# Token mixes of an RWKV-7 layer: residual moved out of memory for a while, second low-rank factors in three rounded passes between the passes of the next mix, operand splits released feature tile by feature tile

## What is computed

```python
x_prev = concatenate([shift0[:, None, :], h[:, :-1]], axis=1)
xx = x_prev - h
xr, xw, xk, xv, xa, xg = [h + xx * mix[i] for i in range(6)]
r = xr @ w_r
k = xk @ w_k
v = xv @ w_v
w_log = -softplus(-(w0 + tanh(xw @ w1) @ w2)) - 0.5
a = sigmoid(a0 + (xa @ a1) @ a2)
g = sigmoid(xg @ g1) @ g2
```

## Time and profile before

| | |
|---|---|
| time, median of 3 | 3700.47 us (3700.26 to 3702.83) |
| the profiled execution's own time | 3682.67 us |
| its span | 3680.8 us |
| mean granted TensorE clock | 0.93 of full |
| busy: PE, PEld, DVE, ACT, POOL | 87%, 81%, 33%, 24%, 30% of the span |
| DMA | 239 MB, 65 GB/s on the mean |

### The profile page before, as it was taken

One profiled execution on the slowest core, in us unless ns is written; L12 is line 12 of the kernel. 1 busy time (PEld: TensorE's weight loads), 2 busy tenths in 40 slices (PEclk: granted clock), 3 DMA queues, 4 the chain that ended last, 5 costly groups with the idle time before them and its releaser, 6 DMA issues.

```text
span 3680.8 us, 70255 instructions
## 1 busy us (share of the span) xinstructions
PE 3217.4 (87%) x30137; PEld 2972.9 (81%) x30137; DVE 1206.9 (33%) x1468; ACT 876.6 (24%) x1355; POOL 1094.3 (30%) x788
## 2 busy tenths in 40 slices
PE   5999968879999999957988588998728899999996
PEld 4989746869999999935988577777528799999995
DVE  4123254151111111364222256666351411111115
ACT  4122334231101101134111245455222201001102
POOL 1323210312332332201222445555303132332331
PEclk8999988889999999968999789999869999999998
DMA  2353542201111111104222212221121011111111
GB/s 77 108 131 105 151 135 79 92 23 37 51 48 40 50 52 34 38 28 143 81 80 80 77 46 54 65 63 46 34 104 46 26 49 34 54 48 37 51 44 56
DMA packets 336604, 239.11 MB, mean 65 GB/s; under 512 B 43527, under 2 KB 311251, under 8 KB 335900
## 3 DMA queue, kind: packets, MB, share of 16 engines
q1 hardware_dynamic: 316490, 191.77, 18.4%
q10 hardware_dynamic: 19922, 44.51, 3.2%
HBM read 177.13 MB, written 58.82 MB: 64 GB/s over the span
## 4 chain that ended last, share of the span: by engine, by line
PE 74%; DVE 11%; issue 6%; ACT 4%; DMA 2%; POOL 2%; SPq 1%; ACTq 0%; DVEq 0%; POOLq 0%
PE PS L435 52%; PE PS L1066 7%; DVE act_lo L375 2%; PE PS L2020 2%; PE PS L2025 2%; DVE hf L399 1%; PE PS L1385 1%; DVE xT L403 1%; PE PS L1763 1%; PE PS L2085 1%; DMA fx_F<-frow 1%; PE PS L2037 1%; PE PS L1409 1%; PE PS L1393 1%; PE PS L1463 1%
## 5 line engine op out<-in xcount | busy, mean ns | idle before, releaser
L416 POOL CAST w_hi<-w_raw 128x1024 fp32r<-128x1024 f32 (+2 forms) x252 | 221.0, 877 | 2077.0 <-PE PS L435 1530.0
L435 PE MATMUL PS<-act_hi,w_hi 128*128 128x344 f32 x3168 | 687.6, 326 | 99.3 <-DVE act_lo L375 77.2
L435 PE MATMUL PS<-act_lo,w_hi 128*128 128x344 f32 x3168 | 679.9, 323 | 0.0
L435 PE MATMUL PS<-act_hi,w_lo 128*128 128x344 f32 x3168 | 675.1, 322 | 0.0
L435 PEld LDWEIGHTS PS<-act_hi,w_hi 128*128 128x128 f32 x3168 | 539.1, 191 | 116.8 <-issue 77.7
L435 PEld LDWEIGHTS PS<-act_lo,w_hi 128*128 128x128 f32 x3168 | 544.0, 192 | 0.0
L435 PEld LDWEIGHTS PS<-act_hi,w_lo 128*128 128x128 f32 x3168 | 534.1, 190 | 0.0
L418 POOL TENSOR_TENSOR w_lo<-w_raw,w_hi 128x1024 fp32r<-128x1024 f32 (+2 forms) x252 | 507.9, 2016 | 20.2
L549 DVE TENSOR_TENSOR hf<-PS,sg 128x1032 f32<-128x1032 f32 x44 | 54.2, 1232 | 798.7 <-PE PS L435 798.7
L435 PE MATMUL PS<-hid_hi,w_hi 128*128 128x344 f32 x1056 | 224.0, 321 | 4.9 <-DVE hid_lo L551 4.9
L435 PE MATMUL PS<-hid_lo,w_hi 128*128 128x344 f32 x1056 | 224.8, 321 | 0.0
(11 more groups left out here) (449 smaller groups left out, 4128.6 us busy)
## 6 DMA issues: line engine op xcount, KB each, us to landing
rw<-stage ACTq DMA_DIRECT2D x48, 516.0 KB, 2.7
w_raw<-in_ffn_w_gate_dram SPq DMA_DIRECT2D x44, 512.0 KB, 3.8
w_raw<-in_ffn_w_up_dram SPq DMA_DIRECT2D x44, 512.0 KB, 3.8
w_raw<-in_ffn_w_down_dram SPq DMA_DIRECT2D x80, 256.0 KB, 2.7
proj<-stage ACTq DMA_DIRECT2D x24, 516.0 KB, 2.7
w_raw<-in_hyb_w_in_dram SPq DMA_DIRECT2D x24, 512.0 KB, 3.8
oT<-mix SPq DMA_DIRECT2D x8, 1032.0 KB, 9.0
x_in<-in_x_prompt_dram SPq DMA_DIRECT2D x2, 2048.0 KB, 7.9
```

Source lines behind the costliest of these rows:

```text
L416: nc.gpsimd.tensor_copy(w_hi[:, u, 0:kts, :], w_raw[:, u, 0:kts, :]).then_inc(w_hi_done, 1)
L435: mm = nc.tensor.matmul(PS[:, 3 * u + c, 0:CH], w[:, u, kt, :], x[:, kt, CH * c:CH * c + CH], start=(kt == 0 and part == 0), stop=(kt == k ...
```

## The change

The residual's memory is given a name, `base_xT`. After the add of layer 0, SP stores xT to DRAM (`xkeep`, 2 of its 8 rows and then 6), and loads it back during the scan (at k == 2); the add for n == 5 waits for that. In between the place of xT holds lora_hi, lora_lo and six staging tiles z_st.

w1 and a1 are loaded side by side as the 128 columns of one weight tile, w2 and a2 as its 128 rows in the other slot; g1 and g2 in the same way one after another. POOL splits the second factors too. ACT rounds `lora` to lora_hi (`rounded`), DVE makes lora_lo, and the second factor is made in three rounded passes of 3 matmuls each (`second`), with 64 or 128 rows, into one set of banks (u = 1). The order of TensorE is: first factor of w; then the first factor of a, with the 8 second-factor tiles of w between its passes; then that of g, with the second factor of a; then r's first output tile, with the second factor of g; then the other tiles of r, k and v.

The splits of the activations no longer wait for the whole previous mix: feature tile k of mix n+1 is written when pass k of the last output tile of mix n is done (`act_free`, `act_used`). ACT's instructions are interleaved by hand, one cast and one copy-out (`keep`) in turn.

The diff, cut; removed lines that stand in the listing above are left out, indentation is reduced by 8:

```diff
...
 ident = sb("ident", [P, P])
 ones = sb("ones", [P, P])
-xT = sb("xT", [P, KT, T])
+base_xT = take(KT * T * 4)
+xT = nc.alloc_sbuf_tensor_at("xT", [P, KT, T], F32, offset=base_xT)
...
-for m in "wag":
-    step(f"a_{m}", 1, 0)
+step("a_wa", 1, 1)
+step("a_g", 1, 1)
 for m in "rkv":
     step(f"a_{m}", 4, 4)
...
     dve.wait_ge(rstd_ready, n + 1 + START)
+    if n == 5:
+        dve.wait_ge(x_back, 16 + START)
...
+x_kept = [sem("x_kept0"), sem("x_kept1")]
+lora_hi, lora_lo = (nc.alloc_sbuf_tensor_at(n, [P, T], F32R, offset=base_xT + i * ROW) for i, n in enumerate(("lora_hi", "lora_lo")))
+NZ = 6
+z_st = [nc.alloc_sbuf_tensor_at(f"z_st{i}", [P, T], F32, offset=base_xT + (2 + i) * ROW) for i in range(NZ)]
+z_out = [sem(f"z_out{i}") for i in range(NZ)]
+xkeep = dram("xkeep", [P, KT * T])
 MIXES = (("w", 1), ("a", 4), ("g", 5), ("r", 0), ("k", 2), ("v", 3))
...
+LORA = (("w", "wa", slice(0, 64), ACT.Tanh, "s"), ("a", "wa", slice(64, 128), ACT.Copy, "a"),
+        ("g", "g", slice(0, 128), ACT.Sigmoid, "g"))
...
+by_tile = lambda name: io[name][0].rearrange("r (j n) -> r j n", n=P)
+def act_free(eng, n, k):
+    name = (LORA[n][1] if n < 3 else MIXES[n][0])
+    if n == 0 and k == KT - 1:
+        eng.wait_ge(lora_full, 1 + START)
+    elif k == KT - 1:
+        u, count = (0, 1) if n < 3 else (1, 4)
+        eng.wait_ge(psum_full[u], plan[f"a_{name}"][u] + count + START)
+    else:
+        eng.wait_ge(act_used, (KT - 1) * (n + (n >= 3)) + k + 1 + START)
...
 def mixes_sync(sp):
...
+    k0, k1 = plan["a_wa"]
+    w1 = w_raw[:, 0, :, :]
+    sp.wait_ge(w_split[0], k0 + START)
+    sp.dma_start(w1[:, :, 0:64], kt_of("rwkv_w1")).then_inc(w1_loaded, 16)
+    sp.dma_start(w1[:, :, 64:128], kt_of("rwkv_a1")).then_inc(w_loaded[0], 16)
+    sp.wait_ge(w_split[1], k1 + START)
+    sp.dma_start(w_raw[0:64, 1, :, :], by_tile("rwkv_w2")).then_inc(w2_loaded, 16)
+    sp.dma_start(w_raw[64:128, 1, :, :], by_tile("rwkv_a2")).then_inc(w_loaded[1], 16)
+    sp.wait_ge(x_ready, 2 * KT + START)
+    for i, rows in enumerate((slice(0, 2), slice(2, KT))):
+        sp.dma_start(xkeep[:, rows.start * T:rows.stop * T], xT[:, rows, :].rearrange("p k t -> p (k t)")).then_inc(x_kept[i], 16)
+    k0, k1 = plan["a_g"]
+    load_w(sp, 0, k0, kt_of("rwkv_g1"))
+    load_w(sp, 1, k1, by_tile("rwkv_g2"))
+    for m in "rkv":
+        load_pairs(sp, f"a_{m}", 4, kt_of("rwkv_w_" + m))
+def mixes_gpsimd(pool):
+    k0, k1 = plan["a_wa"]
+    pool.wait_ge(w1_loaded, 16 + START)
+    split_w(pool, 0, k0, KT, k0 + k1 + 1)
+    pool.wait_ge(w2_loaded, 16 + START)
+    split_w(pool, 1, k1, KT, k0 + k1 + 2)
+    k0, k1 = plan["a_g"]
+    split_w(pool, 0, k0, KT, k0 + k1 + 1)
+    split_w(pool, 0, k0 + 1, KT, k0 + k1 + 2)
+    split_w(pool, 1, k1, KT, k0 + k1 + 3)
+    split_w(pool, 1, k1 + 1, KT, k0 + k1 + 4)
...
+def mixes_tensor(pe):
+    def tile(n, u, k, full, also=lambda kt: None):
+        pe.wait_ge(w_split[u], k + 1 + START)
+        pe.wait_ge(psum_free[u], k + START)
...
+            mm.then_inc(full if kt == KT - 1 else act_used, 1)
+            also(kt)
+    def second(n, j):
+        rows = LORA[n][2]
...
+        if KT * n + j:
+            pe.wait_ge(z_free, KT * n + j + START)
+        for part, (w, x) in enumerate(((w_hi, lora_hi), (w_hi, lora_lo), (w_lo, lora_hi))):
+            for c in range(NCH):
+                mm = nc.tensor.matmul(PS[:, 3 + c, 0:CH], w[rows, 1, j, :], x[rows, CH * c:CH * c + CH],
+                                      start=(part == 0), stop=(part == 2))
+        mm.then_inc(z_full, 1)
+    def between(n):
+        def also(kt):
+            if kt >= 1:
+                second(n, kt - 1)
+            if kt == KT - 1:
+                second(n, kt)
+        return also
+    tile(0, 0, plan["a_wa"][0], lora_full)
+    pe.wait_ge(lora_free, 1 + START)
+    tile(1, 0, plan["a_wa"][0], psum_full[0], between(0))
+    tile(2, 0, plan["a_g"][0], psum_full[0], between(1))
+    for n in (3, 4, 5):
+        k0, k1 = plan[f"a_{MIXES[n][0]}"]
+        if n == 3:
+            tile(n, 0, k0, psum_full[0], between(2))
+            tile_products(pe, 1, k1, act_hi, act_lo, KT, act_ready, KT * (R0 + n))
+        with pe.Fori(1 if n == 3 else 0, 3) as i:
+            tile_products(pe, 0, k0 + i, act_hi, act_lo, KT, act_ready, KT * (R0 + n))
+            tile_products(pe, 1, k1 + i, act_hi, act_lo, KT, act_ready, KT * (R0 + n))
+        tile_products(pe, 0, k0 + 3, act_hi, act_lo, KT, act_ready, KT * (R0 + n))
+        if n < 5:
+            tile(n, 1, k1 + 3, psum_full[1])
         else:
...
+            tile_products(pe, 1, k1 + 3, act_hi, act_lo, KT, act_ready, KT * (R0 + n))
 def mixes_scalar(act):
...
+    def hi(n, ks):
+        for k in ks:
+            act.wait_ge(hf_ready, KT * (made(R0) + n) + k + 1 + START)
+            if n:
+                act_free(act, n - 1, k)
+            nc.scalar.copy(act_hi[:, k, :], hf[:, k % 2, :]).then_inc(hi_ready, 1)
+    def first(n):
+        m, pair, rows, func, _ = LORA[n]
+        k0 = plan[f"a_{pair}"][0]
...
+        if n == 2:
+            act.wait_ge(lora_ready, 2 + START)
+        done, count = (lora_free, 1) if n == 0 else (psum_free[0], k0 + 1)
+        nc.scalar.activation(chunks(lora[:, :])[rows], PS[rows, 0:3, 0:CH], func).then_inc(done, 1)
+        act.wait_ge(done, count + START)
+    def rounded(n):
+        rows = LORA[n][2]
+        if n == 0:
+            act.wait_ge(x_kept[0], 16 + START)
+            act.wait_ge(h_ready, KT + START)
+        if n == 2:
+            act.wait_ge(z_full, 2 * KT + START)
+        nc.scalar.copy(lora_hi[rows, :], lora[rows, :]).then_inc(lora_hi_ready, 1)
+    def keep(n, j):
+        m, _, _, _, out = LORA[n]
+        q = KT * n + j
+        act.wait_ge(z_full, q + 1 + START)
+        if q == 0:
+            act.wait_ge(x_kept[1], 16 + START)
+        if q >= NZ:
+            act.wait_ge(z_out[q % NZ], 16 * (q // NZ) + START)
+        dst = chunks(z_st[q % NZ][:, :])
...
+        ins.then_inc(z_free, 1)
+        act.wait_ge(z_free, q + 1 + START)
+        act.dma_start(rw[RW[out] + P * j:RW[out] + P * j + P, :], z_st[q % NZ][:, :]).then_inc(z_out[q % NZ], 16)
+        if n >= 1 and j == KT - 1:
+            act.sem_inc(psum_full[1], 1)
+            act.sem_inc(psum_free[1], 1)
...
+    hi(0, range(KT))
+    for n in range(3):
+        hi(n + 1, [0])
+        first(n)
+        if n:
+            keep(n - 1, KT - 2)
+        hi(n + 1, [1])
+        rounded(n)
+        if n:
+            keep(n - 1, KT - 1)
+        for k in range(2, KT):
+            hi(n + 1, [k])
+            keep(n, k - 2)
+    for n in (3, 4, 5):
...
+        if n == 3:
+            store(n, 0, 0, k[0], fixed(0, 0))
+            keep(2, KT - 2)
+            keep(2, KT - 1)
+            store(n, 1, 0, k[1], fixed(0, 1))
...
+        store(n, 0, 3, k[0], fixed(3, 0))
+        if n < 5:
+            hi(n + 1, range(4))
+        store(n, 1, 3, k[1], fixed(3, 1))
+        if n < 5:
+            hi(n + 1, range(4, KT))
 def mixes_vector(dve):
...
+    h0, a0 = KT * made(R0), KT * R0
+    for g in range(KT * len(MIXES) + 1):
+        if g < KT * len(MIXES):
+            k, i = g % KT, MIXES[g // KT][1]
+            if g >= 2:
+                dve.wait_ge(act_ready, a0 + g - 1 + START)
+            nc.vector.scalar_tensor_tensor(hf[:, k % 2, :], xx[:, k, :], vec("rwkv_mix", KT * i + k), oT[:, k, :],
+                                           ALU.mult, ALU.add).then_inc(hf_ready, 1)
+        if g >= 1:
+            n, k = divmod(g - 1, KT)
+            dve.wait_ge(hf_ready, h0 + g + START)
+            dve.wait_ge(hi_ready, a0 + g + START)
+            if n:
+                act_free(dve, n - 1, k)
+            nc.vector.tensor_tensor(act_lo[:, k, :], hf[:, k % 2, :], act_hi[:, k, :].bitcast(F32), ALU.subtract).then_inc(act_ready, 1)
+            if 1 <= n <= 3 and k == 1:
+                rows = LORA[n - 1][2]
+                dve.wait_ge(lora_hi_ready, n + START)
+                nc.vector.tensor_tensor(lora_lo[rows, :], lora[rows, :], lora_hi[rows, :].bitcast(F32), ALU.subtract).then_inc(lora_ready, 1)
...
+        if k == 2:
+            sp.dma_start(xT[:, :, :].rearrange("p k t -> p (k t)"), xkeep[:, :]).then_inc(x_back, 16)
...
```

More of the change, by code:

```diff
@@ L1769, in mixes_scalar @@
-        def mixes_scalar(act):
-            stores = S0
-            for n, (m, _) in enumerate(MIXES):
-                r = R0 + n
-                if n:
-                    for u in range(2):
-                        act.wait_ge(psum_full[u], plan[f"a_{m}"][u] + START)
-                split_scalar(act, r)
-                if m not in LORA:
-                    store_scalar(act, f"a_{m}", 4, rw, RW[m], stores)
-                    stores += 4
-                    continue
-                _, _, rank, func, out = LORA[m]
-                k0 = plan[f"a_{m}"][0]
-                act.wait_ge(psum_full[0], k0 + 1 + START)
+            k0, k1 = plan["a_wa"]
@@ L1785, in mixes_scalar @@
```

(36 more changed lines are left out.)

81 lines of the change are left out of this document (29 added, 52 removed).

## The result

| | before | after |
|---|---|---|
| median of the runs, us | 3700.36 (3688.95 to 3702.83, 4 runs) | 3641.93 (3638.97 to 3653.91, 4 runs) |
| ratio to before | | 0.9858, 95% interval 0.9832 to 0.9884 |
| profiled execution, us | 3682.67 | 3638.97 |
| its span, its mean granted clock | 3680.8, 0.932 | 3637.2, 0.943 |
| first pass of w to start of the last copy-out of v | 438.3 | 392.9 |

The kernel is 1.4% faster. Between the two profiled executions the difference is 43.7 us (predicted 43.0); between the medians it is 58.4 us, so the forecast of 3657.5 lies 15.6 us too high, and the result is only 0.9 us over the low end of the range. That 43.7 comes so close to 43.0 is in part luck: it holds a rest that was 2.7 us shorter and an add that began 1.1 us later, and the forecast had neither.

The account below looks back on a forecast made before the run. Mostly PE bound the kernel, with serial second factors and each mix's restart exposed. Threading -26.9, turns -18.4 and residual add +2.3 gave -43.0 us, from the 3700.5 median to 3657.5; own range 3645 to 3670, 8 in 10 3641 to 3683.

Parts of the forecast that it names:

- a's and g's threaded tiles: First-factor tiles of a and g with the previous mix's second-factor passes between: 30.2 us each.
- r's threaded tile: r's first output tile with g's second factor threaded in, waiting for POOL's weight splits: 41.7 us.
- loop of two steps: In threaded tiles, second-factor pass, copy-out, issue, cast, subtraction, tile's pass: 7.07 us for two steps, 3.54 each.
- the two turns: Starts of k and v: splits follow the last tile's passes, each turn costs 4.2 instead of 13.4 us; 18.4 less.
- The threading: From w's first pass to r's second tile, second factors threaded between other passes: 123.5 against 150.4 us, 26.9 less.
- the floor: A 64-row second-factor pass priced at 1.42 us like a 128-row one; upper end 1.85.
- DVE against POOL: DVE loses 2.9 us per POOL weight split beside it; 2.3 us more at the residual add.
- 12.5 in all: If DVE and POOL did not hinder each other at all, the terms would fall by 12.5 us.
- Moved data: Residual's 4.2 MB stored and reloaded, 16 to 36 us each way, taken as covered: zero; up to 36 us if not.
- PE is the pace: Rival, chance 0.12: in threaded tiles ACT and DVE run ahead, a step costs 2.84 us, 12.6 less: 3645.
- The low clock in the threaded tiles: Rival, chance 0.17: threaded steps take 5.44 us, 15.2 more a tile; one tile 3672.7, two 3688.
- The slower one: Rival, chance 0.04: low clock outlasts the threading, 45.6 us through r's threaded tile, 11.3 per plain tile; 3782 with r's seven.

Follow-up runs that it names:

- after again: The kernel after, unchanged, measured again on another chip against before: 3638.26 us, ratio 0.9854.
- the two kernels that isolate them: Kernel after with the new order at the turns to k and v taken out: 3666.61 us; kernel before with only that order put in: 3674.18 us.
- the eight parts: Residual copied back in eight parts behind eight items' loads: on the kernel after 3644.10 us; on that with three further edits 3628.75 us.
- by other means: Kernel before with w's and a's second-factor matmuls contracting over 128 rows instead of 64, lora's lower half zero: 3676.10 us, ratio 0.9956.
- the second profile: The kernel before, unchanged, run once more on another chip for its profile: 3686.76 us.
- the last kernel: Kernel after with first split held back, cast ahead of copy-out, weights' signal moved, and residual copied back in eight parts: 3628.75 us, ratio 0.9823 to before.
- the three edits: Kernel after with POOL's first split held back, cast ahead of copy-out, and weights' signal moved: 3627.29 us, ratio 0.9830 to before.

## Why the prediction was right, and where it was wrong

| step | predicted, us | measured, us |
|---|---|---|
| w's tile | 19.0 | 20.0 |
| a's and g's threaded tiles | 30.2 each | 32.0, 31.6; after again 30.8, 30.6 |
| r's threaded tile | 41.7 | 38.3; after again 39.4 |
| cold start of r's plain tiles | 2.4 | 2.7 |
| loop of two steps, 64 rows / 128 rows | 7.07 | 7.39 / 7.08 |
| the two turns | -18.4 | -17.0, -20.5 |
| first pass of w to last copy-out | -45.3 | -45.4 |
| residual add | +2.3 | +3.5 (2.1 to 3.5) |
| residual moved | 0 | out 0, back +3 to +7 |
| medians | -43.0 | -58.4 |

- **The threading.** The loop was as written, and the last column's 7.08 is from 1723.74 to 1730.82 us in r's tile. For w's and a's factors "the floor" of 1.42 us a pass was too low: 1.62, which is inside the bounds of 1.42 and 1.85. The two tiles with 64 rows came 3.2 us longer together in the first profile and 1.0 in the second; the difference is mainly the low clock around the change of tiles. r's tile came 3.4 and 2.3 us shorter: PE began g's factor 4.7 and 5.4 us after pass 1, where I had 7.1. The errors cancel, which is luck.
- **The turns** were right in each of the two kernels that isolate them.
- **DVE against POOL.** One split costs DVE 2.9 us at the turn to k, as taken. By the rule of the Trainium skill (SBUF — State Buffer, Two separate sides) it would be 3.4. At the add I allowed for less than a whole split, but the split of w2 and a2 fell on it, and 2.1 to 3.5 us went there. The "12.5 in all" that I gave for no hindrance at all is not covered by the terms I wrote down: they name 2.9 us at each turn and 2.3 at the add, so 8.1.
- **Moved data.** "I put both at zero" was right for the way out and wrong for the way back. I asked only who waits for the data, and forgot that 4.1 MB at once may hinder others. That item was long in every profile with the single transfer, and of the items beside the eight parts none took more than 34.8 us; what it was in PE's path that came late is not in the trace.
- **The size for the median: the step that failed** is the last one, carrying the difference of one profiled execution over to the median of the runs. "a's ran at the full level" was true of that execution, which was 17.8 us faster than the median, and untrue of the two other profiles of such a factor. The change removes both 64-row factors, and with them up to 10.6 us more of low clock than I had credited. With both brought to the full level by other means, before becomes 20 us faster, more than the 13 us that w's alone had room for. How many of before's executions have a's factor at the low level is not shown, and it is not all that sets the median apart: the second profile had it low and still took 3686.8 us. The remaining 5 us to the 15.6 are not settled; the range of before's own executions is 34 us.
- **The rivals.** "PE is the pace" did not come in this kernel, and did once the written order was changed. "The low clock in the threaded tiles" occurred within the steps in one of the ten profiles with threaded tiles, for four passes. The slower one didn't occur. The Trainium skill (TensorE: Matmul & The Clock Gate, What's actually happening) has activity release the throttle; here PE was busy without a gap for 27.85 us at 0.50 with 64 rows, and the same count of matmuls with 128 rows was back at the full level within the stretch. The earlier trace rows has a 64-row stretch at the full level too; so the rule, as I read it, does not cover these matmuls. The slower rival's price of 11.3 us a plain tile is a little high: by the 2.72 us a pass of the earlier trace rows it is 10.4, which leaves the rival slower all the same.

**Better than both** is the last kernel, or the one with the three edits: 12 timings of the two have their mean at 3627.5 us, 8 of the kernel after at 3641.7. But they ran on other chips, on which before was faster too (3689.69 and 3692.03 against 3700.36 and 3694.48): beside their own before the two gain 62 and 63 us, the kernel after 58 and 56, so some 5 us remain. The ratios are 0.983 and 0.982 against 0.985 and 0.986, with intervals that overlap. The stages of their profiles (388.6 and 388.8 against 399.3 and 398.6) are 10 us shorter; that the whole of it reaches the total is not shown.

## What to carry to other kernels

Before a difference of one profiled execution is applied to a median, look whether a stretch runs at one of two clock levels, and in which of them the median's executions are likely to run: such a stretch is worth more to remove than its profile shows. When short work is threaded between other work, write down the loop through the in-order engine, and put the cast that feeds the next pass ahead of the copy-out of the last. A large transfer that nobody waits for can still cost its neighbours; cutting it into parts is worth trying, though no total here shows a gain.
